# First even mixer of a two-block network: gate product turned round, decay and square root moved behind the values, way back's quarters and norm reordered

## The reference, cut to what matters

```python
def ab_mixer(xn, w_in, ...):
    proj = xn @ w_in
    xa, ga, qk, v, o, i_pre, f_pre = jnp.split(proj, cuts, axis=-1)   # i_pre, f_pre: 4 columns each
    ya = jax.nn.gelu(ga) * rglru(causal_dwconv(xa, ...), ...)
    yb = mlstm_block(qk, v, o, i_pre, f_pre, ...)
    return jnp.concatenate([ya, yb], axis=-1) @ w_out
# rglru: a = exp(log_a); u = sqrt(-expm1(2 * log_a)) * (ig * x); h = scan of h = a * h + u
# mlstm_block: silu(conv) -> q, k; log_i = i_pre + b_i; log_f = log_sigmoid(f_pre + b_f); two chunks of 128 tokens;
#   weights exp(-(m - d)) on q k^T, a state (k w)^T v carried from chunk 0 to chunk 1, h / max(|den|, exp(-m)), rms norm,
#   sigmoid(o) * h
```

## Time and profile before

| | |
|---|---|
| median of 3 executions | 2307.24 us (2304.0 to 2309.72) |
| the profiled execution | 2304.17 us, of which the span from first to last instruction is 2302.4 us |
| mean granted TensorE clock | 0.98 of full |
| busy share of the span | TensorE 96%, weight loads 82%, VectorE 71%, ScalarE 56%, GpSimd 5% |
| DMA | 362.99 MB, mean 158 GB/s |

### The profile page before, as it was taken

How to read it: one execution, slowest core, us unless ns; L and a number is a source line. 1 busy time by engine, 2 the same in 40 slices (tenths; PEclk the granted TensorE clock), 3 DMA queues, 4 the chain that set the end, 5 groups by cost and what they waited for, 6 DMA issues and landing times.

```text
span 2302.4 us, 33700 instructions
## 1 busy us (share of the span) xinstructions
PE 2202.2 (96%) x12449; PEld 1880.8 (82%) x12449; DVE 1632.7 (71%) x2945; ACT 1283.6 (56%) x2141; POOL 125.1 (5%) x67
## 2 busy tenths in 40 slices
PE   7999999999999999999799999999999999879998
PEld 6888888888888966888688797878887888768886
DVE  6877678778777554877677666577777777558775
ACT  5655766555554265655465565456555555346553
POOL 0001000000003210000000001100010002210001
PEclk9999999999999999999899989999999999989999
DMA  6553245554553421554355331145535553325552
GB/s 250 189 198 132 106 174 184 187 187 181 190 187 138 173 81 57 182 192 174 130 200 192 140 129 48 56 148 200 192 142 201 192 192 115 129 82 184 187 206 78
DMA packets 64653, 362.99 MB, mean 158 GB/s; under 512 B 7464, under 2 KB 8232, under 8 KB 32488
## 3 DMA queue, kind: packets, MB, share of 16 engines
q1 hardware_dynamic: 64064, 360.31, 43.0%
q10 hardware_dynamic: 296, 0.27, 0.0%
q0 software_dynamic: 128, 0.26, 0.0%
HBM read 359.76 MB, written 1.05 MB: 157 GB/s over the span
## 4 chain that ended last, share of the span: by engine, by line
PE 79%; DVE 12%; ACT 6%; issue 1%; DMA 1%; POOL 0%; DVEq 0%; SPq 0%; ACTq 0%; POOLq 0%
PE ps L196 77%; DVE WL L120 5%; ACT work L186 3%; PE ps L201 2%; ACT WH L186 2%; DVE work L120 2%; DVE work L131 1%; ACT XBt L186 1%; DVE XBt L131 1%; DMA ring<-wts 1%; DVE small L131 1%; DVE small L120 1%; DVE work L125 0%; DVE Xt L131 0%; ACT L186 0%
## 5 line engine op out<-in xcount | busy, mean ns | idle before, releaser
L196 PE MATMUL ps<-XBt,WH 128*128 128x512 f32 (+1 forms) x4192 | 1218.2, 357 | 20.4 <-DVE XBt L131 14.3
L120 DVE TENSOR_TENSOR WL<-ring,WH 128x1024 fp32r<-128x1024 f32 x624 | 771.3, 1236 | 310.8 <-ACT WH L186 264.9
L186 ACT ACTIVATE WH<-ring 128x1024 fp32r<-128x1024 f32 x663 | 702.3, 1059 | 392.6 <-PE ps L196 329.8
L196 PE MATMUL ps<-XBt,WL 128*128 128x256 f32 x3376 | 897.6, 281 | 0.0
L196 PEld LDWEIGHTS ps<-XBt,WH 128*128 128x128 f32 x4192 | 734.5, 192 | 128.3 <-DVE XBt L131 20.6
L196 PEld LDWEIGHTS ps<-XBt,WL 128*128 128x128 f32 x3376 | 644.3, 191 | 26.2
L196 PE MATMUL ps<-WH,HHt 128*128 128x512 f32 x712 | 279.9, 393 | 6.1 <-ACT HHt L186 5.2
L196 PE MATMUL ps<-WL,HHt 128*128 128x512 f32 x712 | 277.9, 390 | 0.0
L196 PE MATMUL ps<-WH,HLt 128*128 128x512 f32 x712 | 275.2, 390 | 0.0
L186 ACT ACTIVATE work<-ps 128x256 f32<-128x256 f32 (+5 forms) x443 | 178.9, 405 | 66.2 <-PE ps L196 28.2
L186 ACT ACTIVATE work<-work 128x256 f32<-128x256 f32 (+4 forms) x229 | 103.6, 453 | 199.7 <-DVE work L120 196.3
(11 more groups left out here) (127 smaller groups left out, 1320.7 us busy)
## 6 DMA issues: line engine op xcount, KB each, us to landing
ring<-wts SPq DMA_DIRECT2D x248, 1024.0 KB, 5.8
ring<-wts SPq DMA_DIRECT2D x180, 512.0 KB, 3.8
ring<-wts SPq DMA_DIRECT2D x1, 1152.0 KB, 5.1
ct<-cons SPq DMA_DIRECT2D x1, 1086.5 KB, 12.0
Xt<-x SPq DMA_DIRECT2D x4, 256.0 KB, 4.7
out<-Xt SPq DMA_DIRECT2D x1, 1024.0 KB, 4.0
ring<-wts SPq DMA_DIRECT2D x2, 256.0 KB, 2.6
ring<-wts SPq DMA_DIRECT2D x1, 288.0 KB, 2.8
```

Source lines behind the costliest of these rows:

```text
L120: self.done(self.e and self.e.tensor_tensor(out, a, b, op), inc)
L186: self.done(self.e and self.e.activation(out, a, f, **kw), inc)
L196: inst = self.e and self.e.matmul(out, l, r, start=start, stop=stop)
```

## The change

Seven edits in the mixer's lists:

1. The gate product is turned round: the 8 gate columns are the stationary side and XH, XL move (24 matmuls with 256 moving columns). The result, 8x256, is copied to SBUF by ScalarE (IFR), and `if_turn_pe` turns it back with two transposes, behind ab_q.0.
2. In ScalarE's and VectorE's lists the gates' small steps stand behind ab_q.0's taps instead of ahead of them.
3. `gates_pe` stands ahead of `rows_pe`.
4. `decay_act` stands behind KW instead of ahead of the silus; its square (AL by AL) is made by VectorE.
5. The Relu of EX is made by VectorE (TENSOR_SCALAR, subtract then max) instead of ScalarE.
6. The root, the recurrence's scans and the two gelus stand later; rows of ab_g.1 stand ahead of YA's first half.
7. On the way back quarters 0 and 1 of n = 0 are followed by `results_pe`, then both quarters of n = 1; `lo` of ab_w0.0 stands behind the norm, and `hi` and `lo` of ab_w0.1 stand between the two halves of the gated results.

```diff
+                for kt in range(8):
+                    c = slice(kt * 8, kt * 8 + 8)
+                    P.mm3(ps["ab_if"][0:8, 0:256], wif[:, c], wil[:, c], XH[:, kt, :], XL[:, kt, :], kt == 0, kt == 7,
+                          inc="ab_if" if kt == 7 else None)
+                ps.give("ab_if", "ab.ifr")
+
+            def if_turn_pe(P):
+
+                ps.take("ab.ift")
+                P.wait_ge("ab.ifr", *ps.free("ab.ift"))
+                P.mm(ps["ab.ift"][:, 16:24], ONES[0:4, :], dib[0:4, :], True, True)
+                for i in range(2):
+                    P.tr(ps["ab.ift"][:, i * 8:i * 8 + 8], IFR[0:8, hs(i)], IDN[0:8, 0:8], inc="ab.ift" if i else None)
+                ps.give("ab.ift", "ab.ife")
...
                 cm_pe(P, "ab_q.0", t)
+                if_turn_pe(P)
                 cm_pe(P, "ab_q.1", t)
                 cm_pe(P, "ab_k.0", t)
+                gates_pe(P)
                 rows_pe(P)
-                gates_pe(P)
...
                     for i in range(2):
                         first_pe(P, n, i)
-                results_pe(P)
-                for n in range(2):
                     for i in range(2):
                         out_quarter(P, t, 1, n, i)
+                    if not n:
+                        results_pe(P)
...
-                A.act(fl(UU), fl(AL), ACT.Square, inc="ab.al", back=5)
...
                 taps_act(A, "ab_x.1")
...
+                A.wait_ge("ab_if")
+                A.act(IFR[0:8, :], ps["ab_if"][0:8, 0:256], ACT.Copy, inc="ab.ifr")
+                hi(A, ahead("ab_q.0"))
+                taps_act(A, "ab_q.0")
+                A.wait_ge(f"{t}.nr", "ab.ift")
...
                 softplus_act(A, t, 2, g1, g2, g3)
-                hi(A, ahead("ab_q.0"))
-                taps_act(A, "ab_q.0")
...
-                decay_act(A)
                 silu_of(A, "ab_q.0")
                 silu_of(A, "ab_q.1")
                 silu_of(A, "ab_k.0")
...
-                        A.act(EX[c][:, hs(h)], ps[f"ab.m{c}"][:, hs(h)], ACT.Relu, bias=NC[:, c * 4 + h:c * 4 + h + 1],
...
-                A.wait_ge("ab.uu")
-                A.act(fl(UU), fl(UU), ACT.Sqrt, scale=-1.0, inc="ab.sq1")
...
+                decay_act(A)
                 hi(A, ahead("ab_g.0"))
-                gated_act(A, "ab_g.0", GA, ACT.Gelu_apprx_tanh)
...
+                A.wait_ge("ab.uu")
+                A.act(fl(UU), fl(UU), ACT.Sqrt, scale=-1.0, inc="ab.sq1")
                 hi(A, ahead("ab_g.1"))
-                gated_act(A, "ab_g.1", GA, ACT.Gelu_apprx_tanh)
+                for q in range(2):
+                    gated_act(A, f"ab_g.{q}", GA, ACT.Gelu_apprx_tanh)
...
+                in_act(A, t, 1, Y8, "ab.ya1", "ab_o.1")
                 hi(A, ahead("ab_o.1"))
-                in_act(A, t, 1, Y8, "ab.ya1", "ab_o.1")
                 gated_act(A, "ab_o.1", OO, ACT.Sigmoid)
                 for i in range(2):
+                    hi(A, ahead("ab_w0.0"), (i,))
...
+                for c in range(2):
+                    V.wait_ge(f"ab.m{c}")
+                    for h in range(4):
+                        V.ts(EX[c][:, hs(h)], ps[f"ab.m{c}"][:, hs(h)], NC[:, c * 4 + h:c * 4 + h + 1], 0.0, SUB, MAX,
...
+                V.wait_ge("ab.al")
+                V.tt(fl(UU), fl(AL), fl(AL), MUL)
+                V.stt(fl(UU), fl(UU), 1.0, fl(T1), ADD, MUL, inc="ab.uu")
+                rows_dve(V, "ab_g.0", GA[:, 0:2, :])
+                lo(V, ahead("ab_g.0"))
                 V.wait_ge("ab.sq1")
                 V.stt(fl(UU), fl(UU), 0.5, fl(GX), MUL, MUL)
                 for c in range(4):
                     V.scan(XC[:, c, :], AL[:, c, :], UU[:, c, :], 0.0, MUL, ADD, back=min(c + 1, 4))
...
+                rows_dve(V, "ab_g.1", GA[:, 2:4, :])
+                lo(V, ahead("ab_g.1"))
                 V.wait_ge("ab_g.0.th")
                 V.tt(YA[:, 0:2, :], GA[:, 0:2, :], XC[:, 0:2, :], MUL, inc="ab.ya0")
...
                 rows_dve(V, "ab_o.0", OO[:, 0:2, :])
-                lo(V, ahead("ab_o.0"))
                 V.wait_ge("ab.hs")
...
                 V.tt(y4, y4, dd, MUL)
+                lo(V, ahead("ab_o.0"))
+                in_dve(V, t, 1, Y8)
+                lo(V, ahead("ab_o.1"), (0,))
...
                 for i in range(2):
                     back_dve(V, i)
+                    lo(V, ahead("ab_w0.0"), (i,))
                     back_lo_dve(V, i)
-                lo(V, ahead("ab_w0.0"))
```

More of the change, by code:

```diff
@@ L1009, in ab_mixer @@
             YA, YB = Y8[:, 0:4, :], Y8[:, 4:8, :]
-            R = lambda i, a=0, b=256: at(4096 + i * 256, 256)[0:4, a:b]
+            R = lambda i, a=0, b=256, n=4: at(4096 + i * 256, 256)[0:n, a:b]
             R34 = at(4096, 512)[0:4, :]
@@ L1020, in ab_mixer @@
             V1 = at(17960, 1032).rearrange("p (i h e) -> p i h e", i=2, h=4)
-            IFT = v3(sm(16), 2)
+            IFT, IFR = v3(sm(16), 2), R(5, n=8)
             IT, NF, SP, g1, g2, g3, BC = [sm(8) for _ in range(7)]
@@ L1039, in if_pe @@
                 P.wait_ge("ab_if:lo", *ps.free("ab_if"))
-                P.mm(ps["ab_if"][:, 16:24], ONES[0:4, :], dib[0:4, :], True, True)
+                for kt in range(8):
[7 more added lines that the diff above has]
+                P.mm(ps["ab.ift"][:, 16:24], ONES[0:4, :], dib[0:4, :], True, True)
                 for i in range(2):
[L1042 to L1045, removed]
+                    P.tr(ps["ab.ift"][:, i * 8:i * 8 + 8], IFR[0:8, hs(i)], IDN[0:8, 0:8], inc="ab.ift" if i else None)
+                ps.give("ab.ift", "ab.ife")
             def rows_pe(P):
@@ L1215, in decay_act @@
                 for c in range(4):
-                    A.act(T1[:, c, :], T1[:, c, :], ACT.Tanh, scale=c4[:, c:c + 1], bias=c4[:, c:c + 1], back=4)
-                A.act(fl(UU), fl(AL), ACT.Square, inc="ab.al", back=5)
+                    A.act(T1[:, c, :], T1[:, c, :], ACT.Tanh, scale=c4[:, c:c + 1], bias=c4[:, c:c + 1], inc="ab.al" if c == 3 else None,
+                          back=4)
             def gated_act(A, piece, D, f):
@@ L1233, in act @@
                 taps_act(A, "ab_x.1")
-                A.wait_ge(f"{t}.nr", "ab_if")
-                A.act(BC, ps["ab_if"][:, 16:24], ACT.Copy)
+                A.wait_ge("ab_if")
[3 more added lines that the diff above has]
+                A.wait_ge(f"{t}.nr", "ab.ift")
+                A.act(BC, ps["ab.ift"][:, 16:24], ACT.Copy)
                 for i in range(2):
-                    A.act(IFT[:, i, :], ps["ab_if"][:, i * 8:i * 8 + 8], ACT.Copy, scale=n_r[:, i:i + 1], inc="ab.ife" if i else None,
+                    A.act(IFT[:, i, :], ps["ab.ift"][:, i * 8:i * 8 + 8], ACT.Copy, scale=n_r[:, i:i + 1], inc="ab.ife" if i else None,
                           back=2)
@@ L1259, in act @@
                 silu_of(A, "ab_k.0")
[L1260 to L1263, removed]
-                        A.act(EX[c][:, hs(h)], ps[f"ab.m{c}"][:, hs(h)], ACT.Relu, bias=NC[:, c * 4 + h:c * 4 + h + 1],
-                              inc=f"ab.m{c}.e" if h == 3 else None, back=4 if h else 1)
                 silu_of(A, "ab_k.1")
@@ L1268, in act @@
                 for c in range(2):
-                    A.act(EX[c], EX[c], ACT.Exp, scale=-1.0, inc=f"ab.ex{c}", back=3)
-                A.wait_ge("ab.uu")
-                A.act(fl(UU), fl(UU), ACT.Sqrt, scale=-1.0, inc="ab.sq1")
+                    A.wait_ge(f"ab.m{c}.e")
+                    A.act(EX[c], EX[c], ACT.Exp, scale=-1.0, inc=f"ab.ex{c}")
                 A.wait_ge("ab.v1")
@@ L1301, in act @@
                 gated_act(A, "ab_o.0", OO, ACT.Sigmoid)
+                in_act(A, t, 1, Y8, "ab.ya1", "ab_o.1")
                 hi(A, ahead("ab_o.1"))
-                in_act(A, t, 1, Y8, "ab.ya1", "ab_o.1")
                 gated_act(A, "ab_o.1", OO, ACT.Sigmoid)
                 for i in range(2):
+                    hi(A, ahead("ab_w0.0"), (i,))
                     A.wait_ge(f"ab.yb{i}")
                     A.act(XH[:, 4:8, hs(i)], YB[:, :, hs(i)], ACT.Copy, inc=f"ab.yhb{i}")
-                hi(A, ahead("ab_w0.0"))
                 hi(A, ahead("ab_w1.0"))
@@ L1360, in dve @@
                 taps_dve(V, "ab_x.1")
+                conv_rows_dve(V, "ab_q.0")
+                lo(V, ahead("ab_q.0"))
+                taps_dve(V, "ab_q.0")
                 V.wait_ge("ab.ife")
@@ L1365, in dve @@
                 softplus_dve(V, t, 1, SP, NF, g1, g2, g3)
[L1366 to L1369, removed]
                 conv_rows_dve(V, "ab_q.1")
                 lo(V, ahead("ab_q.1"))
+                softplus_dve(V, t, 2, SP, NF, g1, g2, g3, inc="ab.sp")
                 taps_dve(V, "ab_q.1")
@@ L1376, in dve @@
                 V.wait_ge("ab.cl")
-                V.ts(NC, ps["ab.cl"][:, 0:8], -1.0, None, MUL, None, inc="ab.nc")
+                V.cp(NC, ps["ab.cl"][:, 0:8], inc="ab.nc")
                 V.wait_ge("ab.r4")
@@ L1389, in dve @@
                 V.stt(fl(GX), fl(GX), 1.0, fl(XC), ADD, MUL)
-                V.wait_ge("ab.al")
```

(18 more changed lines are left out.)

## The result

The changed kernel takes 2294.77 us in the median (2290.9 to 2295.03, 4 executions), the kernel before 2307.2 us (2304.0 to 2309.72, 4 executions). The ratio is 0.9943, with a 95% interval of 0.9926 to 0.996: 12.4 us faster, where 9.3 was forecast. The profiled executions differ by a little more: 2290.9 against 2304.17 us, and their spans, 2289.1 against 2302.4, by 13.3.

What follows compares the result with a forecast made beforehand. TensorE, busy 96% of the span, was taken as the bound, so only its idle time or slow matmuls could be won. The mixer's way back starting its second half at 317.2, not 326.5, gave 9.3 us: 2297.9 us, range 2291.5 to 2304.5.

Steps and rivals of the forecast that it cites:

- Gate product, ab_q.0: TensorE at the gates: turned product 2.9 us plus 0.4 turn, saving 4.7; ab_q.0 behind it at full clock saves 2.5.
- Rival A: Gate product: the clock falls all the same, with only 8 stationary columns in use; gain 4.8 us, 2302.4; chance 0.14.
- rival E: Gate product's time is hidden anyway and new idle time takes the rest: no change, 2307; chance 0.03.
- ab.r5: VectorE's result behind the softplus: comes at new 253.6, 5.0 us earlier than before.
- End of ab_g.0's split: ScalarE, with decay, square and Relus moved out of this part: the split ends at new 268.3, not 280.04.
- The new wait: TensorE ahead of quarter 0: idle for 5.5 us, longer than any wait before, until new 303.3.
- Rival D: From the new idle time ahead of quarter 0 TensorE stays at 1.2 GHz: 8 us slower, 2315; chance 0.05.
- Rival B: Chain to quarter 0 comes later, two hand-offs missing: idle time grows to 10 us, gain 4.3, 2302.9; chance 0.10.
- The second half of the way back: Mixer's way back: its second half starts at new 317.2 instead of 326.5, giving the 9.3 us gain.
- rival C: Chain to quarter 0 is shorter: restart at full clock, hand-offs free; gain 13 us, 2294.3; chance 0.10.
- Gates ahead of rows cost nothing: TensorE's list up to ab_k.1: both inputs are ready, so the new order brings no stall; no gain priced.
- Out go 4.05 + 1.04 + 2.38: ScalarE from ab.r5 to ab_g.0's split: decay, square and Relus leave its 21.4 us; about 0.8 of waiting comes back.

Runs made afterwards that it cites:

- the doubled product: The changed kernel with its turned gate product made twice (48 products, the second overwriting the first): 2299.15 us, ratio 0.997.
- the run with the old middle: The changed kernel with decay, square, Relu, root, scans and gelus back in their old places, gate product and way back as changed: 2294.68 us, ratio 0.9955.

## Why the prediction was right, and which of its reasons were not

The forecast of 9.3 us was the way through the mixer, and that got 9.4 shorter. The execution after came to the gate product 222.91 - 220.77 = 2.1 us earlier than the one before, ahead of anything that the change touches: 0.6 by an earlier start of the mixer's matmuls (205.13, not 205.70) and the rest by ab_x.1's clock. With 2.1 added to its times, the terms came out so:

- **Gate product, ab_q.0.** 2.9 and 5.8 us were forecast, 2.80 and 5.84 measured at full clock; the turn took 0.44 (0.4). Rival A is out, by the profile and by the doubled product; rival E (the time is hidden anyway) is out, since the old product costs 7.8 us in the changed kernel.
- **ab.r5** at 253.6: it ends at 251.18 + 0.41 = 251.59, + 2.1 = 253.7. **End of ab_g.0's split** at 268.3: 264.06 + 2.15 = 266.21, + 2.1 = 268.3. **Relus** 2.3: 2.36.
- **The new wait** of 5.5 us ahead of quarter 0 at 303.3: 5.35, at 301.43 + 2.1 = 303.5. The restart was priced at 1.6; quarter 0's first 12 products took 4.72 us at a mean clock of 0.61, and 2.9 in the run that came to them without a wait: 1.8. Rival D, a clock that stays low, fell: behind it the row at 306.15 shows 1.00. Rival B, a wait of 10 us, did not come either.
- **The second half of the way back** at 317.2: in the profile after it starts at about 315.1, + 2.1 = 317.2.
- **DMA** was no wait of TensorE anywhere in the mixer.

The median of 2294.77 us itself lies just below the forecast's own range (2295 to 2301) and next to rival C's 2294.3, yet C's reason is not what happened: the restart was slow, as priced. And 9.4 against 9.3 is closer than one pair of profiles can tell, with restarts that differ by 0.9 us; so far the agreement is luck, while the terms above, each within some 0.3 us, are not.

What was wrong is how I shared the gain out, since the sum never had to say what an edit is worth alone. The steps on TensorE's way, each by its own profiles: edits 1 and 2 2.4 us, edit 3 4.1 more, edit 7 1.9 more (106.37 to 104.46), edits 4 to 6 1.0 more; together 9.4. The last is no larger than restarts differ by. Edit 2 without edit 1, and edits 4 and 6 each alone, were not tried.

- "Gates ahead of rows cost nothing" was true, but I gave edit 3 no worth. It covers the wait for the softplus: with edits 1 and 2 TensorE reaches the rows 7.0 us earlier (243.36 - 222.51 = 20.85 us behind the first mark, not 250.72 - 222.91 = 27.81), while the softplus, which edit 2 puts later in the lists, ends 1.1 us later than before (22.8 behind the mark, not 21.8). Without edit 3 ab_k.1 ends 5.4 us later: 2.0 by waiting, the rest mostly by half clock in the products behind. VectorE takes up ab_k.1 4.1 us later for it, and 4.1 or 3.7 us are lost at the end of the way. Of the 5.0 us by which ab.r5 came earlier, 2.4 reached the end without edit 3.
- "Out go 4.05 + 1.04 + 2.38" from ScalarE is right as bookkeeping, and the two waits went as I said. But the chain to the root got longer by the same decay (the square's wait of 2.45 us above), and TensorE got the time back as one wait ahead of quarter 0. Net 1.0 us, not a main term.
- A single edit's loss depends on the others: without the turned gate product edits 2 to 7 save 1.6 us (112.87 - 111.30); with it the sum is 9.4, where it and edit 2 alone have 2.4.

**The rest of the 12.4 or 13.3 us** no run here puts down to the change. Of the 13.3 between the profiled executions 9.4 are the way, 1.8 lie behind it and 2.1 ahead of it. Of these, 0.6 us came ahead of the mixer's matmuls and about 1.5 from ab_x.1: from the end of the unchanged wait of 1.8 us ahead of it to the gate product are 6.3 to 6.4 us in eight of the fourteen profiles and 7.8 to 7.9 in the other six, among them kernels with the same instructions up to there. The part behind the mixer, the same code in all fourteen, took 1966.6 us before and 1964.9 after, and between 1964.8 and 1973.8 in the other profiles. With 9 us of such spread, medians can order kernels 3 us apart by chance. But the medians give most kernels more than the way does (edits 1 and 2: 4.9 and 2.4; edits 1, 2 and 3: 7.8 and 6.5; edit 3 undone: 9.1 and 5.7), and the way before is known from one execution alone. So whether the true gain is nearer 9 or 12 stays open; against the 2305.1 us of the kernel before in the other sets, the changed kernel's median would be some 10 us faster.

## What to carry to other kernels

Cost a change along each engine's list, not by what it takes from the busiest one: work taken off one wait often stands as one wait further on, and a profile with that edit undone says what it is worth. Move an order edit together with what makes it needed: here the turned product paid 2.4 us until the products behind it were put in the order in which their inputs come. Measure an edit in one stage between two marks of the trace when the rest of the program varies by more than the edit, and in more than one execution when the edit is worth about 1 us.

## What the runs showed that I had not expected

- Products with 8 stationary and 256 moving columns held full clock for 48 in a row (5.6 us), while products with 128 stationary and 8 moving columns lost it within their own run in both profiles that have them (mean clock 0.70 and 0.71), although by the profile TensorE is 100% busy in all of them. The Trainium skill ("TensorE: Matmul & The Clock Gate", "What's actually happening") has the gate follow how busy the engine has been; by the rows here the profile's busy share does not tell the two apart.
- Behind a wait of 2.0 us in front of small products the gates ran at half clock for most of their 6.3 us (mean 0.56), while behind the same small products without a wait they took 3.7 us in the kernel before, at full clock; in the run with the old middle a wait of 2.3 us in front of the state's products left the clock full and one of 4.0 us in front of k's transposes did not (busy time by stretch of that run, behind the wait of 4.0 and behind that of 2.3). The same wait of 1.8 us ahead of ab_x.1 led to either level from one profile to the next, worth 1.5 us.

```profile
270.89:276.00 5.11, 5.11 (x31) 5.11 (x32) 3.47 (x4) 5.03 (x6) 0.00 (x0) 0.67 0.09 29
282.95:286.50 3.55, 3.55 (x30) 3.55 (x31) 3.21 (x4) 3.38 (x3) 0.00 (x0) 1.00 0.31 67
```
